# Two heads at a time in half of TensorE's array: the small matmuls of an indexed sparse attention, paired by head

## The reference, cut to what matters

```python
# indexer, per block of 128 queries
sc = relu(einsum('bthd,bsd->bths', iq, ik))       # 8 heads, d = 64, one shared key
score = einsum('bths,bth->bts', sc, iw)
_, idx = top_k(where(causal, score, -inf), 64)
# attention over the selected keys
logits = einsum('bthd,btkhd->bthk', q, k_sel) * 64 ** -0.5 + rel_bias[bucket]
probs = softmax(where(valid, logits, -inf))
out = einsum('bthk,btkhd->bthd', probs, v_sel)
```

## Time and profile before

| | |
|---|---|
| time, median of 3 runs | 918.39 us |
| the profiled execution, its own time | 917.69 us |
| its span, first to last instruction | 915.9 us |
| PE busy | 880.1 us, 96% |
| DVE busy | 683.6 us, 75% |
| ACT busy | 450.2 us, 49% |
| mean DMA rate | 219 GB/s |
| granted TensorE clock, mean | 0.994 of full speed |

### The profile page before, as it was taken

The page is one execution under the profiler, slowest core; times in us unless marked ns, Lnnn a source line. Parts: engine busy times, 40 slices in busy tenths (PEclk is TensorE's granted clock), DMA queues, the critical chain, the costliest instruction groups (busy, mean ns, idle before and its releaser), DMA issues.

```text
span 915.9 us, 14506 instructions
## 1 busy us (share of the span) xinstructions
PE 880.1 (96%) x5776; PEld 760.4 (83%) x5776; DVE 683.6 (75%) x1084; ACT 450.2 (49%) x712; POOL 70.3 (8%) x64
## 2 busy tenths in 40 slices
PE   8999999999999799989999999989999899999996
PEld 7988887667876697779989999868987799999995
DVE  4697788786996887779867767886787876646666
ACT  5563544444545644455544544354554555444550
POOL 2000001000000110011111010010000120100101
PEclk9999999999999999999999999999999999999999
DMA  8855566544957680399957787648724885665601
GB/s 287 325 170 168 201 202 228 167 143 158 325 207 302 233 318 24 120 345 312 378 184 265 265 323 269 219 152 326 234 93 176 335 309 184 204 201 160 208 3 47
DMA packets 56893, 200.74 MB, mean 219 GB/s; under 512 B 6589, under 2 KB 7925, under 8 KB 56825
## 3 DMA queue, kind: packets, MB, share of 16 engines
q1 hardware_dynamic: 55816, 196.63, 61.4%
q0 software_dynamic: 1008, 3.18, 0.9%
HBM read 198.71 MB, written 1.08 MB: 218 GB/s over the span
## 4 chain that ended last, share of the span: by engine, by line
PE 89%; DVE 6%; issue 2%; ACT 1%; DMA 1%; POOL 1%; SPq 0%; DVEq 0%; ACTq 0%
PE ps L1099 27%; PE ps L1100 26%; PE ps L1101 26%; PE ps L1272 3%; PE ps L1293 1%; PE ps L1112 1%; PE ps L1279 1%; DMA ring<-in_w_iq 1%; PE ps L1233 1%; DVE wk L1366 1%; PE ps L1261 1%; DVE X L1763 1%; PE ps L1191 1%; DVE small L1768 0%; PE ps L1253 0%
## 5 line engine op out<-in xcount | busy, mean ns | idle before, releaser
L1099 PE MATMUL ps<-XT,wsp 128*128 128x256 f32 x768 | 217.2, 283 | 4.3 <-DVE XT L1373 3.0
L1100 PE MATMUL ps<-XT,wsp 128*128 128x256 f32 x768 | 214.6, 279 | 0.0
L1101 PE MATMUL ps<-XT,wsp 128*128 128x256 f32 x768 | 214.2, 279 | 0.0
L1330 DVE TENSOR_TENSOR wsp<-ring,wsp 128x1024 fp32r<-128x1024 f32 x130 | 160.5, 1241 | 17.6 <-ACT wsp L1861 17.6
L1861 ACT CAST wsp<-ring 128x1024 fp32r<-128x1024 f32 (+1 forms) x129 | 134.6, 1046 | 64.6 <-PE ps L1101 52.1
L1099 PEld LDWEIGHTS ps<-XT,wsp 128*128 128x128 f32 x768 | 144.0, 188 | 8.5 <-issue 4.2
L1100 PEld LDWEIGHTS ps<-XT,wsp 128*128 128x128 f32 x768 | 144.0, 188 | 0.9
L1101 PEld LDWEIGHTS ps<-XT,wsp 128*128 128x128 f32 x768 | 143.6, 187 | 0.0
L1099 PE MATMUL ps<-wsp,ra 128*128 128x512 f32 x236 | 95.2, 403 | 6.9 <-issue 5.1
L1101 PE MATMUL ps<-wsp,ra 128*128 128x512 f32 x236 | 94.3, 399 | 0.0
L1330 DVE TENSOR_TENSOR wsp<-arena,wsp 128x1024 fp32r<-128x1024 f32 x74 | 92.6, 1256 | 1.7 <-ACT wsp L1861 1.7
(11 more groups left out here) (263 smaller groups left out, 1554.4 us busy)
## 6 DMA issues: line engine op xcount, KB each, us to landing
arena<-in_mod_w SPq DMA_DIRECT2D x48, 512.0 KB, 5.7
ring<-in_mod_w SPq DMA_DIRECT2D x44, 512.0 KB, 4.8
ring<-in_ffn_a SPq DMA_DIRECT2D x30, 512.0 KB, 5.1
arena<-in_ffn_b SPq DMA_DIRECT2D x28, 512.0 KB, 4.8
ring<-in_ffn_o SPq DMA_DIRECT2D x27, 512.0 KB, 4.5
arena<-in_ffn_o SPq DMA_DIRECT2D x17, 512.0 KB, 4.9
ring<-in_ffn_b SPq DMA_DIRECT2D x16, 512.0 KB, 5.1
ring<-in_w_moz SPq DMA_DIRECT2D x14, 512.0 KB, 3.6
```

Source lines behind the costliest of these rows:

```text
L1099: pe.matmul(o, l[0], r[0], start=start, stop=False)
L1100: pe.matmul(o, l[0], r[1], start=False, stop=False)
L1101: return pe.matmul(o, l[1], r[0], start=False, stop=stop)
L1330: ve.tensor_tensor(w[:, 1024:1024 + n], raw[slot[0]][:, 0:n], w[:, 0:n].bitcast(f32), SUB).then_inc(*done("V", "lo", u, also=[("raw", *slo ...
```

## The change

The DSA's steps are counted anew: `of("dsa", i)` gives head i // 4 * 2 + i % 2 and query block i // 2 % 2, so steps i and i + 1 (i even) are two neighbouring heads of the same query block, an even and an odd one. A new step `sc2` at even i emits on PE the logits of both: two matmuls over 64 rows, one in rows 0 to 63 and one in rows 64 to 127 and each into its own bank, then the two bias matmuls. A new step `pv2` emits the value products of both, key block by key block with the two heads alternating, into partitions 0 to 63 and 64 to 127 of one bank. On PE the order within a step is now `pv2`, `tp`, `sc2`, where it was `sc`, `tp`, `pv`. The indexer's PE part `ix_p` runs for four heads at once, the even ones into one bank and the odd ones into another; ACT and DVE still go by two heads. Step for step, DVE and ACT do what they did before, for other heads and sizes. SP and POOL have the same instructions in the same order.

```diff
+def of(task, i):
+
+    return (i // 4 * 2 + i % 2, i // 2 % 2) if task == "dsa" else (i // 2, i % 2)
...
     def indexer():
         for t in range(2):
             for g in range(4):
-                b, s = bank.get(), wk.get()
-                add("ix_s", t, g, b, prior("bank", b), s, prior("wk", s))
+                if g % 2 == 0:
+                    bs = [bank.get(), bank.get()]
+                    add("ix_p", t, g, bs, [prior("bank", b) for b in bs])
+                b, s = bs[g % 2], wk.get()
+                add("ix_s", t, g, b, s, prior("wk", s))
                 bank.put(b[0])
                 wk.put(s[0])
                 yield
...
+    def dsa_steps():
+
+
+        lag, n = 3, 16
+        ps, pts, bs, out = {}, {}, {}, None
+        for i in range(n + lag + 2):
+            q = i - lag - 3
+            if q >= 0 and q % 2 == 0:
+                if q % 4 == 0:
+                    out = bank.get()
+                add("pv2", q, out, prior("bank", out), [pts[q], pts[q + 1]], q % 4 == 2)
+                for e in range(2):
+                    pt.put(pts[q + e][0])
+                if q % 4 == 2:
+                    fin_dsa(q // 4, out)
+                    bank.put(out[0])
+            if 0 <= i - lag < n:
+                q = i - lag
+                b, pts[q] = bank.get(), pt.get()
+                add("tp", "dsa", q, b, prior("bank", b), ps[q], pts[q], prior("pt", pts[q]))
+                bank.put(b[0])
+                pb.put(ps[q][0])
+            if i < n:
+                if i % 2 == 0:
+                    bs = {i + e: bank.get() for e in range(2)}
+                    add("sc2", i, [bs[i], bs[i + 1]], [prior("bank", bs[i + e]) for e in range(2)])
+                ps[i] = pb.get()
+                add("sc", "dsa", i, bs[i], None, ps[i], prior("pb", ps[i]))
+                bank.put(bs[i][0])
+            if 0 <= i - 1 < n:
+                add("norm", "dsa", i - 1, ps[i - 1])
             yield
 
...
-                elif kind == "ix_s":
-                    t, g, b, before, s, _ = a
+                elif kind == "ix_p":
+                    t, g, bs, before = a
                     n = 128 * (t + 1)
-                    for e_, h in enumerate(((0, 2), (1, 3), (4, 6), (5, 7))[g]):
+                    for h in range(2 * g, 2 * g + 4):
                         for e in new("P", ("iq", h // 2), ("iq", 4), before):
                             pe.wait_ge(*e)
-                        r = slice(64 * (h % 2), 64 * (h % 2) + 64)
-                        ins = pe.matmul(ps[b[0]][:, e_ * n:(e_ + 1) * n], iqT[r, h // 2, t * 128:(t + 1) * 128],
+                        r, c = slice(64 * (h % 2), 64 * (h % 2) + 64), h // 2 % 2
+                        ins = pe.matmul(ps[bs[h % 2][0]][:, c * n:(c + 1) * n], iqT[r, h // 2, t * 128:(t + 1) * 128],
                                         ikT[r, 0:n], start=True, stop=True)
-                    ins.then_inc(*done("P", "fill", *b))
+                        if c:
+                            ins.then_inc(*done("P", "fill", *bs[h % 2]))
...
+                elif kind == "sc2":
+                    i, bs, before = a
+                    for e_, b in enumerate(bs):
+                        n, [(l, r, events)] = head("dsa", i + e_)
+                        for e in new("P", events, before):
+                            pe.wait_ge(*e)
+                        pe.matmul(ps[b[0]][:, 0:n], l, r, start=True, stop=False)
+                    for e_, b in enumerate(bs):
+                        for e in new("P", ("tb",), ("misc",)):
+                            pe.wait_ge(*e)
+                        pe.matmul(ps[b[0]][:, 0:n], anti, TB[:, of("dsa", i + e_)[0], 256 - n:256].bitcast(f32),
+                                  start=False, stop=True).then_inc(*done("P", "fill", *b))
+                elif kind == "sc" and a[0] != "dsa":
                     task, i, b, before = a[0:4]
                     n, terms = head(task, i)
-                    if task == "dsa":
-                        terms.append((anti, TB[:, i // 2, 256 - n:256].bitcast(f32), [("tb",), ("misc",)]))
...
-                    for j in range(i % 2 + 1):
+                    for j in range(of(task, i)[1] + 1):
                         ins = pe.transpose(ps[b[0]][:, j * 128:(j + 1) * 128], pb[s[0]][:, j * 128:(j + 1) * 128], ID)
                     ins.then_inc(*done("P", "fill", *b, also=[("pb", *s)]))
+                elif kind == "pv2":
+                    i, b, before, ds, ends = a
+                    t = of("dsa", i)[1]
+                    for j in range(t + 1):
+                        for e_, d in enumerate(ds):
+                            h = of("dsa", i + e_)[0]
+                            for e in new("P", ("tp", "dsa", i + e_), ("av", j), before):
+                                pe.wait_ge(*e)
+                            ins = pe.matmul(ps[b[0]][64 * e_:64 * e_ + 64, t * 128:(t + 1) * 128],
+                                            av[:, j, h * 64:(h + 1) * 64], pt[d[0]][:, j * 128:(j + 1) * 128],
+                                            start=j == 0, stop=j == t)
+                    freed = [("pt", *d) for d in ds]
+                    if ends:
+                        ins.then_inc(*done("P", "fill", *b, also=freed))
+                    else:
+                        ins.then_inc(*done("P", "pv", "dsa", i, also=freed))
                 elif kind == "pv":
                     task, i, b, before, d, ends = a
                     h, t = i // 2, i % 2
-                    dh = 64 if task == "dsa" else 128
-                    r0 = (h % (128 // dh)) * dh
                     for j in range(t + 1):
-                        if task == "dsa":
-                            l, event = av[:, j, h * 64:(h + 1) * 64], ("av", j)
-                        else:
-                            l, event = vv[:, j, h * 128:(h + 1) * 128], ("v", int(task == "moba"), j, h // 4)
-                        for e in new("P", ("tp", task, i), event, before):
+                        for e in new("P", ("tp", task, i), ("v", int(task == "moba"), j, h // 4), before):
                             pe.wait_ge(*e)
-                        ins = pe.matmul(ps[b[0]][r0:r0 + dh, t * 128:(t + 1) * 128], l,
+                        ins = pe.matmul(ps[b[0]][:, t * 128:(t + 1) * 128], vv[:, j, h * 128:(h + 1) * 128],
                                         pt[d[0]][:, j * 128:(j + 1) * 128], start=j == 0, stop=j == t)
```

More of the change, by code:

```diff
@@ L536, in order, with attention @@
         more_raw(("ml_o", 3, 1))
-    def attention(task, per, finish, may=lambda h: True):
+    def attention(task, finish, may=lambda h: True):
         lag, n = 3, 16
@@ L558, in attention @@
                 h, t = q // 2, q % 2
-                if t == 0 and h % per == 0:
+                if t == 0:
                     outs["b"] = bank.get()
                 b = outs["b"]
-                ends = t == 1 and h % per == per - 1
-                add("pv", task, q, b, prior("bank", b), pts[q], ends)
+                add("pv", task, q, b, prior("bank", b), pts[q], t == 1)
                 pt.put(pts[q][0])
-                if ends:
-                    finish(h // per, b)
+                if t:
+                    finish(h, b)
                     bank.put(b[0])
+            yield
+    def dsa_steps():
[27 more added lines that the diff above has]
+                add("norm", "dsa", i - 1, ps[i - 1])
             yield
@@ L573, in fin_dsa @@
         wk.put(s[0])
-    def dsa_steps():
-        for _ in attention("dsa", 2, fin_dsa):
-            yield
     proj_b("u", 8, "w_az", 0, 4, lambda j, b: add("ev_az", j, b))
@@ L1263, in tensor @@
                     ins.then_inc(*done("P", "ml_o", h, t, also=[("pb", *x) for x in es] if t else []))
-                elif kind == "sc":
+                elif kind == "sc2":
[11 more added lines that the diff above has]
+                elif kind == "sc" and a[0] != "dsa":
                     task, i, b, before = a[0:4]
                     n, terms = head(task, i)
-                    if task == "dsa":
-                        terms.append((anti, TB[:, i // 2, 256 - n:256].bitcast(f32), [("tb",), ("misc",)]))
                     for q, (l, r, events) in enumerate(terms):
@@ L1940, in scalar @@
                 elif kind == "ix_s":
-                    t, g, b, _, s, before = a
+                    t, g, b, s, before = a
                     n = 128 * (t + 1)
```

16 lines of the change are left out of this document (8 added, 8 removed).

## The result

The changed kernel takes 908.75 us, the median of four runs (907.44 to 909.39). Beside it on the same chip the kernel before took 918.55 us (917.83 to 920.71, four runs). The two medians are 9.8 us apart, which is a ratio of 0.9893. The forecast was 905.5 us in a range of 903.2 to 911.0, with 0.93 on faster. So direction and range held, and the time is 3.25 us above the number named.

A forecast was written before the change was run, and what follows sets the result against it. PE, busy nearly the whole span, was taken as the bound. Its 14.6 us saving less 0.3, 0.9 and 0.5 us of waits left 12.9 us: 904.8 us profiled, 905.5 us as median, range 903.2 to 911.0 us.

The forecast's parts named there:

- The prices of the pieces: PE's small matmuls: 0.105 us a pass per 128 columns, 0.15 to 0.2 us per change of mode, halves overlapping fully.
- Strict order: Rival, chance 0.08: PE keeps program order, only the two inner passes overlap; 2.7 us given back, 908.2 us.
- no overlap: Rival, chance 0.08: row halves on PE do not run at once; 7.9 us stay saved, 910.5 us.
- The sum on PE, 14.6 us: PE time saved: indexer 4.2 us, logits 5.9 us, values 4.5 us.
- Unit 34, 0.3 us: Weight load at 138.72 us already waits for DVE's remainder; 0.3 us of PE's saving taken off.
- The transposes at the mLSTM's first half, 0.9 us: At 190.62 us PE waits for DVE's scaling; the 0.9 us PE saves since 181.43 us counted as lost.
- Other waits, 0.5 us: Behind that wait: busy DVE, probabilities' transposes about 1 us nearer their scaling, logits holding two banks; 0.5 us off.
- Behind the DSA nothing changes and everything moves up together.: After the DSA the order stays the same, so the whole gain was to carry on to the end.
- DVE becomes the bound: Rival, chance 0.05: in the DSA DVE cannot follow, half of its 10.4 us gain (5.2 us) is lost, 910.7 us.
- DVE's waits nearly gone: Sign: DVE's waits for the indexer's relu results (4.8 us) and the DSA's logits (7.4 us) nearly vanish.
- Slower: Rival, chance 0.04: transposes waiting for softmax delay the next logits, 2.4 us in each of eight pairs, 924.7 us.
- does not do what it says: Rival, chance 0.02: halves do not overlap and switching row halves costs 0.20 us like a mode change; 915.7 us.

The follow-up runs named there:

- e4: Changed kernel with the value products of a pair emitted head by head instead of key block by key block: 909.92 us, ratio 0.989.
- e2: Changed kernel with the logits of a pair emitted head by head (half rows, bias, half rows, bias): 913.49 us, ratio 0.9928.
- e7: Changed kernel with the two heads' value products of a pair on either side of the step's transposes: 912.21 us, ratio 0.9924.
- e3: Kernel before with only the indexer's four heads at a time, the DSA as before: 914.57 us, ratio 0.9935.
- e1: Changed kernel with the transposes of the mLSTM's first half two weight units later: 908.03 us, ratio 0.9866.
- e6: Changed kernel with the DSA's pace at 1.25 steps a weight unit instead of 1.53: 908.21 us, ratio 0.9881.
- e12: Changed kernel with the logits of a pair emitted ahead of the transposes of the pair before them: 909.08 us, ratio 0.9895.
- e9: Changed kernel with both the DSA's pace at 1.25 and the later transposes of the mLSTM's first half: 905.92 us, ratio 0.9869.
- e5: Changed kernel with one in four of w_moz's weight remainders made by POOL instead of DVE: 912.32 us, ratio 0.992.
- e11: Kernel before with the DSA's pace at 1.25 steps a weight unit instead of 1.53: 920.67 us, ratio 1.0021.
- e8: Kernel before with one in four of w_moz's weight remainders made by POOL instead of DVE: 921.19 us, ratio 1.0015.
- e10: Changed kernel with POOL's share of DVE's weight remainders set to 0.5 while the gated branch runs: 911.23 us, ratio 0.9925.

## Why the prediction held, and where it was short

**The prices of the pieces.** Right, to 0.03 us each. The overlap of row halves was taken from a row on column halves, and it holds. Strict order and no overlap are out by e4 and by the starts 7 ns apart.

**The sum on PE, 14.6 us.** Right in its parts: logits 5.9 us (e2: 5.9, and 5.7 by its pieces), values 4.5 (e7: 4.1), indexer 4.2 (e3: 3.9 ahead of unit 34). The two in the DSA are not clean measurements of one term, since each also moves the waits; added to e3's 3.5 they give 13.5, more than the 9.6 that all three bring together.

**Unit 34, 0.3 us.** Measured 0.3.

**The transposes at the mLSTM's first half, 0.9 us.** This is the step that was mis-sized. Its mechanism was right: a wait for DVE there, which no change on PE moves. Its size was 3.8 us instead of 0.9: 2.2 us more waiting, and 1.6 us through the clock behind it. Two things were left out. First, I took only what PE saves between 181.43 and 190.62 us as lost. I held DVE's chain fixed in its own start, but PE feeds the whole stretch earlier; DVE has to do the same work in less time from 161 us on, and has 0.74 us in 10 left there. A wait came up at L1326, 1.55 us, that was not in the sum. Second, the three waits were followed by 3.4 us at the lower clock. This was in neither a term nor the range. Nor would more care with the waits have given it: e1 waits 3.7 us and e6 2.6 us in the same stretch at the full clock. The sign "PE's wait grown from 0.46 to about 1.4 us" held at its own place, 1.1 us at the transposes; it is with L1326's wait that it comes to 2.65.

**Other waits, 0.5 us.** Not measured by itself. Between 14.6 us and the lead of 10.0 at 243 us 0.2 us are left, once 0.3 (indexer), 0.3 (unit 34) and 3.8 are off. That is no more than the error of the prices: 0.03 us on each of the eight pairs of logits alone makes 0.24.

**"Behind the DSA nothing changes and everything moves up together."** Nearly. The lead falls by 0.4 us up to 583 us. Then, at an unchanged place, it loses 1.8 us more in the profiled execution. Both kernels wait 2.9 us there for the same operation; only the changed one has a lower clock behind. The wait, and the windows of after and of e6 (the granted clock is 0.72 and 1.00):

```profile
PE ps L1148 <- ACT X L2143: 2.9, 1, 2.9
```

```profile
585.00:597.00 12.00, 9.12 (x61) 5.96 (x54) 8.32 (x17) 5.17 (x8) 1.83 (x2) 0.72 0.14 44
```

```profile
585.00:597.00 12.00, 8.13 (x66) 5.79 (x55) 8.59 (x17) 6.34 (x10) 1.85 (x2) 1.00 0.12 44
```

The lower clock lasts 6.8 us there in the changed kernel, e4 and e12, 3.4 us in e1 and e9, and is absent in before, e2, e3 and e6. Of the others it is 6.8 us in e5, 3.4 us in e7 and e11, and absent in e8 and e10. What decides it is open: all of these kernels run the same instructions there. The profiled execution has the lowest mean clock of the four of its kernel, 0.988; the others have 0.989, 0.991 and 0.992, and the one with 0.992 is the fastest, 907.44 us. An estimate: 0.004 of 907 us is 7 us at half clock, about one such stretch. So some of the four may be without this loss; only one of them has a trace.

**DVE becomes the bound (0.05).** In part what happened. I had put 5.2 us on it for half of the DSA's gain; it took 2.2 us and 1.6 us through the clock. That the time lay in the range all the same owes something to luck: its upper end, 911.0 us, was set by other rivals, and no term held the clock. Rows 8 had DVE at 14.40 of 20 us there, an average over a stretch in which its idle time was PE's to give. The earlier trace rows were read as slack that goes when logits come sooner. They do come sooner, and with them goes the cover of everything else in DVE's queue. The sign "DVE's waits nearly gone" didn't hold: of the 12.2 us of the earlier trace rows 6.1 us are left, 3.1 in the indexer and 3.0 in the DSA.

**Slower (0.04), does not do what it says (0.02).** Out. Scaling is waited for once in eight pairs, 1.6 us, not 2.4 us eight times.

## What to carry to other kernels

Two products that each fill half of the array cost as much as one, in halves of rows or of columns, and the change of mode is then paid once. Work the saving out per piece from the chain of waits; here it came out within 0.03 us a piece. What arrives depends on the engine that feeds the stretch: for each stretch ask how much faster its second-busiest engine could go, and take the gain beyond that off, and keep a microsecond or two in the range for the lower clock that can follow a few short waits. And try anew whatever paced the old pieces: one number in the planner gave a lead of 2 us here in the traces (not clear of noise in the times), where the same number cost 2.8 us before the change.

## What the runs showed of the hardware

- Changing between whole and half array costs about 0.2 us each way, as read ahead of the runs; e2, which only adds such changes and takes the overlap away, confirms the sums with it (1.66 and 2.52 us a pair, where four changes and eight passes make 1.64 and 2.48). Into 64 columns the way in is 0.15 us, as read from the earlier trace rows.
- Float32 matmuls of different halves overlap fully, both passes, also where the program has four records of one half ahead of the other's (0.59 us for eight, e4). The Trainium skill (TensorEngine Tiling (Array Packing), Key Properties) says that a change of tile alone does not drain TensorE; the starts 7 ns apart agree.
- The same 2.9 us wait was followed by 6.8 us at the lower clock, by 3.4 us, or by none, in kernels that run the same instructions around it; it costs up to 1.8 us. So it was at 182 us: 2.65 us of waits, none longer than 1.55 us, with the lower clock behind them, 3.7 us (e1, over 9 us) and 2.6 us (e6) without. No run here tells what decides it. The Trainium skill (TensorE: Matmul & The Clock Gate, A second HAM failure mode: psum-queue depth-cycling) tells of a kernel in which frequent short idle gaps of TensorE made its clock go up and down; these rows show that such gaps are not enough by themselves.
- The traces differ by up to 4.2 us at 61 us, though the kernels run the same instructions up to there. e7 came 3.1 us late against before. 1.7 us of it are there at 15 us, behind longer waits of PE for DVE: the longest is 2.3 us, in front of the first projection matmul (0.85 us in the changed kernel). The rest comes with a stretch at the lower clock, 16.4 to 19.8 us. In this window the changed kernel's clock is 1.00. Whether a kernel or a single execution decides it is not shown:

```profile
14.00:22.00 8.00, 7.04 (x46) 7.07 (x47) 6.29 (x13) 2.04 (x3) 0.00 (x0) 0.79 0.91 313
```

A comparison of two profiles has to take this off before it explains a microsecond.
